# Mixer projections with high and low rows side by side, and GpSimd scaling the gates

## The reference, cut to what matters

```python
def hybrid_mixer(h, w_in, b_forget, g_kv, w_kv_up, g_idx_k, w_up_fox, w_up_sb, w_up_dsa, w_out, cos, sin):
    (q_a, k_a, v_a, f_a, q_b, k_b, v_b, q_c, c_kv, q_i, k_i, w_i, gates) = split(h @ w_in)
    y_a = forgetting_attention(heads(q_a), heads(k_a), heads(v_a), f_a + b_forget)
    y_b = stick_breaking_attention(heads(q_b), heads(k_b), heads(v_b))
    k_c, v_c = split(rmsnorm(c_kv, g_kv) @ w_kv_up, 2)
    ...                                   # rotations, index scores, top-k selection
    y_c = dsa_attention(q_c, k_c, v_c, q_i, k_i, w_i)
    g_a, g_b, g_c = split(sigmoid(gates), 3)
    merged = g_a * (y_a @ w_up_fox) + g_b * (y_b @ w_up_sb) + g_c * (y_c @ w_up_dsa)
    return merged @ w_out

for l in range(2):
    x = x + 0.5 * swiglu(rmsnorm(x, g_ffn1[l]), ...)
    x = x + hybrid_mixer(rmsnorm(x, g_mix[l]), w_in[l], ...)
    x = x + 0.5 * swiglu(rmsnorm(x, g_ffn2[l]), ...)
```

## Time and profile before

| | |
|---|---|
| time, median of 3 runs | 2421.66 us (2421.42 to 2421.71) |
| span of the profiled execution | 2420.2 us, 1.4 us under the median |
| PE busy | 2401.0 us, 99% |
| DVE busy | 1556.3 us, 64% |
| ACT busy | 1216.8 us, 50% |
| POOL busy | 359.8 us, 15% |
| chain that ended last | PE 96%, DVE 2%, ACT 1% |
| PE's granted clock | 0.9 or more of full speed in each of 40 slices |

### The profile page before, as it was taken

One profiled execution on the slowest core, in us unless ns is written; L12 is line 12 of the kernel. 1 busy time (PEld: TensorE's weight loads), 2 busy tenths in 40 slices (PEclk: granted clock), 3 DMA queues, 4 the chain that ended last, 5 costly groups with the idle time before them and its releaser, 6 DMA issues.

```text
span 2420.2 us, 37041 instructions
## 1 busy us (share of the span) xinstructions
PE 2401.0 (99%) x14600; PEld 2057.4 (85%) x14600; DVE 1556.3 (64%) x2659; ACT 1216.8 (50%) x2220; POOL 359.8 (15%) x340
## 2 busy tenths in 40 slices
PE   8999999999999999999999999999999999999998
PEld 6766689888888877988888899998888889999887
DVE  5335455663455556677688677578767767757875
ACT  4344444322222546565566545566656554556654
POOL 0343322000001235200100000240010010024000
PEclk9999999999999999999999999999999999999999
DMA  6334423443454422455655554355565564435554
GB/s 279 132 113 157 157 87 122 160 168 134 157 169 140 152 94 98 149 185 173 203 202 181 180 177 136 117 191 190 171 212 175 175 200 150 148 110 199 190 175 137
DMA packets 88605, 389.96 MB, mean 161 GB/s; under 512 B 15025, under 2 KB 27601, under 8 KB 58353
## 3 DMA queue, kind: packets, MB, share of 16 engines
q1 hardware_dynamic: 81232, 356.07, 43.3%
q0 software_dynamic: 7200, 31.52, 3.7%
HBM read 386.52 MB, written 1.05 MB: 160 GB/s over the span
## 4 chain that ended last, share of the span: by engine, by line
PE 96%; DVE 2%; ACT 1%; issue 0%; DMA 0%; POOL 0%; SPq 0%; DVEq 0%; POOLq 0%; ACTq 0%
PE ps L1243 43%; PE ps L1283 38%; PE ps L1479 3%; PE ps L1542 2%; PE ps L1553 2%; PE ps L1568 2%; PE ps L1377 1%; PE ps L1392 1%; DVE ring_lo L2217 1%; PE ps L1523 0%; ACT logits L1951 0%; DMA arena<-w_mod 0%; PE ps L1346 0%; PE ps L1411 0%; ACT w_hi L1718 0%
## 5 line engine op out<-in xcount | busy, mean ns | idle before, releaser
L2217 DVE TENSOR_TENSOR ring_lo<-ring,w_hi 128x1024 fp32r<-128x1024 f32 (+4 forms) x708 | 777.4, 1124 | 202.8 <-ACT w_hi L1718 200.1
L1718 ACT ACTIVATE w_hi<-ring 128x1024 fp32r<-128x1024 f32 (+4 forms) x708 | 634.3, 944 | 290.0 <-PE ps L1243 199.1
L1243 PE MATMUL ps<-h_hi,w_hi 128*128 128x256 f32 (+1 forms) x1632 | 500.1, 332 | 1.9 <-ACT arena L1841 1.2
L1243 PE MATMUL ps<-h_lo,w_hi 128*128 128x256 f32 (+1 forms) x1632 | 487.9, 324 | 0.1
L1283 PE MATMUL ps<-h_hi,w_hi 128*128 128x512 f32 x1760 | 446.3, 393 | 0.6 <-DVE h_hi L2390 0.3
L1283 PEld LDWEIGHTS ps<-h_hi,w_hi 128*128 128x128 f32 x1760 | 316.2, 189 | 57.6 <-issue 1.5
L1243 PEld LDWEIGHTS ps<-h_hi,w_hi 128*128 128x128 f32 x1632 | 307.1, 190 | 38.3 <-issue 12.2
L1243 PEld LDWEIGHTS ps<-h_lo,w_hi 128*128 128x128 f32 x1632 | 307.5, 190 | 24.2 <-DVE h_lo L2518 0.4
L1243 PE MATMUL ps<-h_hi,ring_lo 128*128 128x256 f32 (+1 forms) x1632 | 307.1, 325 | 0.3 <-DVE ring_lo L2217 0.3
L1243 PEld LDWEIGHTS ps<-h_hi,ring_lo 128*128 128x128 f32 x1632 | 250.3, 190 | 28.5 <-issue 2.2
L1283 PEld LDWEIGHTS ps<-h_hi,ring_lo 128*128 128x128 f32 x1760 | 242.4, 190 | 18.3 <-DVE ring_lo L2217 0.6
(11 more groups left out here) (298 smaller groups left out, 2900.3 us busy)
## 6 DMA issues: line engine op xcount, KB each, us to landing
ring<-w_ffn_in SPq DMA_DIRECT2D x132, 1024.0 KB, 4.8
ring<-w_ffn_out SPq DMA_DIRECT2D x96, 704.0 KB, 4.1
ring<-w_in SPq DMA_DIRECT2D x36, 1024.0 KB, 4.8
ring<-w_w_in SPq DMA_DIRECT2D x26, 1024.0 KB, 4.9
bias_t<-w_mod POOLq DMA_DIRECT2D x24, 1024.0 KB, 5.3
ring<-w_mod SPq DMA_DIRECT2D x16, 1024.0 KB, 6.2
ring<-w_up SPq DMA_DIRECT2D x16, 576.0 KB, 3.7
ring<-w_pab SPq DMA_DIRECT2D x8, 1024.0 KB, 4.9
```

The source lines that it names most:

```text
L1243: mm = pe.matmul(ps[fs[k].bank][:, at_col:at_col + n], (hi_w if wpart == "hi" else lo_w)[0:rows, at[k]:at[k] + P], hi if part == "hi" else ...
L1718: act.activation(w_hi[q.s % 2][:, h * n:(h + 1) * n], ring[q.slot][:, h * n:(h + 1) * n], ACT.Copy)\
L2217: dve.tensor_tensor(ring_lo[q.slot][:, c], ring[q.slot][:, c], plain(w_hi[q.s % 2][:, c]), ALU.subtract)\
```

## The change

In the mixers of the second block the feature and gate tiles now use `product_wide`. So that it finds its rows, the layer ahead writes the mixer's rows side by side ("wide" in place of "defer"), and the token-wise projections read them from there. Per tile there are 8 matmuls of 512 columns and 8 of 256 in place of 24 of 256. The insertions keep about their place in time: the numbers in the tables are changed to count the longer matmuls.

Taking a tile out has new steps. ACT copies columns 256 to 511 of the bank into `spare` (two buffers; it also waits until DVE has taken the tile two before). DVE waits for that copy and adds the halves. For a feature tile DVE then multiplies by `row` in a second instruction that waits for the first. For a gate tile POOL multiplies by `row`, one tile later in its stream, and the Sigmoid waits for it. The gates of branch 1 move from `h_hi` to `h_lo`, since `h_hi` is now full.

```diff
@@ hybrid_kernel
-        gate_lo = over("gates_b", KC * S, h_at + 4 * KC * S, F32)
+        gate_lo = over("gates_b", KC * S, l_at, F32)
@@ feat
+                mix = {}
+                if name[0] == "2":
+                    mix = dict(mix=count("mix"), free=mixed[-2] if len(mixed) > 1 else None, gate=last_gate[0] if name[1] == "g" else None)
+                    mixed.append(f)
+                    if name[1] == "g":
+                        last_gate[0] = (c, f, count("gate_row"))
@@ second_block
-            ffn(w["ffn1_in"][l], w["ffn1_out"][l], "half", None, ("defer", v("g_mix", 8 * l, 8)), fresh=plan.counts["h"],
+            ffn(w["ffn1_in"][l], w["ffn1_out"][l], "half", None, ("wide", v("g_mix", 8 * l, 8)), fresh=plan.counts["h"],
...
-            among(t, lambda: {13: [turned((feat2, 12 * S, 0), 1, fc(12))], 20: [turned((feat2, 13 * S, 0), 0, fc(13))]})
+            among(t, lambda: {7: [turned((feat2, 12 * S, 0), 1, fc(12))], 13: [turned((feat2, 13 * S, 0), 0, fc(13))]})
...
-            among(t, lambda: {12: stick_z(0, 1)})
+            among(t, lambda: {6: stick_z(0, 1)})
...
-            among(t, lambda: {20: stick_z(4)})
+            among(t, lambda: {13: stick_z(4)})
@@ pe_feat
-                if st["tiles"]:
+                if st["tiles"] and st["name"][0] == "2":
+                    product_wide(st["tiles"], [(st["p"], [(c * P * st["n"] + st["i"] * P, h_hi[:, c * SQ:(c + 1) * SQ], c) for c in range(KC)])],
+                                 st["fresh"], mids=st.get("mids", {}))
+                elif st["tiles"]:
@@ act_feat
                 if st["name"][0] == "2":
+                    full(f)
+                    if st["free"]:
+                        taken(st["free"])
+                    act.activation(spare[:, st["mix"] % 2 * S:(st["mix"] % 2 + 1) * S], ps[f.bank][:, S:SQ], ACT.Copy).then_inc(mix_half, 1)
                     return
@@ act_merge2, open_gates
+                    act.wait_ge(gate_row, st["gate_row"] + 16 + m + 1)
@@ gpsimd
+            def gate_by_row(gate):
+                if gate:
+                    c, f, _ = gate
+                    taken(f)
+                    pool.tensor_tensor(gates2(c), gates2(c), row[:, 0:S], ALU.mult).then_inc(gate_row, 1)
@@ dve_feat
-                if not gate and (c < 3 or 6 <= c < 9 or 12 <= c < 15):
-                    ins = dve.scalar_tensor_tensor(dst, ps[f.bank][:, 0:S], SCALE, row[:, 0:S], ALU.mult, ALU.mult)
-                else:
-                    ins = dve.tensor_tensor(dst, ps[f.bank][:, 0:S], row[:, 0:S], ALU.mult)
+                dve.wait_ge(mix_half, st["mix"])
+                ins = dve.tensor_tensor(dst, ps[f.bank][:, 0:S], spare[:, st["mix"] % 2 * S:(st["mix"] % 2 + 1) * S], ALU.add)
+                if not gate:
+                    link(ins)
+                    if c < 3 or 6 <= c < 9 or 12 <= c < 15:
+                        ins = dve.scalar_tensor_tensor(dst, dst, SCALE, row[:, 0:S], ALU.mult, ALU.mult)
+                    else:
+                        ins = dve.tensor_tensor(dst, dst, row[:, 0:S], ALU.mult)
```

More of the change, by code:

```diff
@@ L1209, in run, with within @@
                     mm.then_inc(piece_begun, 1)
+            def within(its):
+                for what, it in its if isinstance(its, list) else [its]:
+                    dict(sums=pe_sums, spread=pe_spread, att=pe_att, head_spread=pe_head_spread, rope=pe_rope, kvup=pe_kvup,
+                         index=pe_index, stick_z=pe_stick_z, unread=lambda u: between(dict(unread=u), 0))[what](it)
             def product(fs, n, groups, fresh=None, need=None, at_col=0, mids={}, more=False, hold=False, odd=None):
@@ L1238, in product @@
                         if at_mm in mids:
[L1239 to L1241 removed]
+                            within(mids[at_mm])
                         at_mm += 1
@@ L1474, in pe_tok @@
                                 c, at = j * per + i, i * cols
-                                for part in parts:
+                                for part in range(1 if low else 2):
                                     if at_mm in mids:
@@ L1478, in pe_tok @@
                                     at_mm += 1
-                                    mm = pe.matmul(ps[f.bank][:, 0:st["n"]], at_T(part, c, T, t * P, P), wt[:, at:at + st["n"]],
-                                                   start=c == 0 and part is h_hi and not low, stop=c == KC - 1 and low)
+                                    rows = at_T(h_hi, c, SQ, part * S + t * P, P) if T == S else at_T(h_lo if part else h_hi, c, T, t * P, P)
+                                    mm = pe.matmul(ps[f.bank][:, 0:st["n"]], rows, wt[:, at:at + st["n"]],
+                                                   start=c == 0 and part == 0 and not low, stop=c == KC - 1 and low)
                                     run(p, mm)
```

40 lines of the change are left out of this document (22 added, 18 removed).

## The result

The changed kernel takes 2436.57 us (median of 5 runs, 2436.32 to 2437.0), the one before 2421.57 us (5 runs beside them, 2421.0 to 2421.71). The ratio is 1.0062, with a 95% interval of 1.0051 to 1.0073: 0.6% slower, 3.2 us above the forecast of 2433.4 and within its range. The profiled execution spans 2434.5 us, 14.3 more than before.

A forecast was written before the change was run, and what follows sets the result against it. PE was taken to set the time nearly everywhere. Waits of 1.35 + 5.95 + 0.4 = 7.7 us a layer, less 1.8 kept in gate tiles, leave 5.9, 11.8 in both: span 2432.0, median 2433.4 us, range 2423 to 2443.

The forecast's parts named there:

- PE's gain: Feature and gate tiles: a row chunk costs 348.4 ns, before 357.9; 9.5 ns less, 6.2 us in all.
- The turn: Turn of chunk 12: three feature tiles' second DVE instructions end L2571 later; PE's rotation waits the whole 1.35 us.
- The stick-breaking chain: Index scores through `va`: copies behind Abs and Exp make masks and splits late; PE waits 5.95 us a layer.
- term 2.1: PE 2.1 us behind at the mask of head 2, the index scores' 0.4 us included.
- term 3.85: Through `va`: PE waits 3.05 us for ACT's split of the second piece, then 0.8 us for DVE's.
- The start of the attention: Among the gate tiles: DVE now waits for the copy as well; 0.4 us a layer (0 to 0.45).
- POOL: Gate tiles: 48 products of about 0.92 us, 22 us a layer, fit; cost put at nothing.
- The contention rival: DVE's splits and POOL's products: ten meet on the critical path at 0.92 us, adding 9 us: 2442.6; chance 0.07.
- The sign that the prediction names: The forecast is wrong if, among other signs, DVE's splits grow longer beside POOL's products.
- What ACT gets: Mixer: 82 copies of 383 ns, 31.4 us; the work fits, but a copy waits for its tile and behind insertions.
- All hidden: Rival: every new step fits into idle time and PE keeps its 6.2 us: 2415.5 us; chance 0.12.
- Only DVE's second instruction: Rival: copies cost nothing further down; PE waits 2.7 us a layer at chunk 12, head 2 and `va`: 2423.5; chance 0.15.

The follow-up runs named there:

- the experiment: Changed kernel with early Sigmoids, tenth gate tile in the old way, only feature tiles 15, 11, 16, 17 in the new: 2419.74 us, ratio 0.9992 to the kernel before.
- the kernel with neither step: Changed kernel without ACT's copies and without DVE's second instruction in the feature tiles: 2417.40 us, ratio 0.9982 to the kernel before.

## Why the forecast held, and which terms were off

- **What bounds the kernel.** Right: PE's stream sets the time, and the loss is idle time that others give it.
- **PE's gain.** The 9.5 ns a row chunk came out somewhat lower: 9.2 between neighbouring gate tiles, 8.5 over all 24 (1.62 us a layer against 1.8). "The feature tiles' own gain is lost in those waits": right. At the turn a part is even seen as such (0.24 us).
- **The turn.** Right in place and cause. The term was 1.35 us and measured 1.39 for the three instructions. PE's lost gain of 0.24 stands on top, as the forecast had counted the gain as lost.
- **The stick-breaking chain.** Right in mechanism: the copy behind Abs and Exp, DVE idle for it, the masks and then both halves of the split late. Undoing only that order brought 8.9 us back. The stretch up to the scores of head 4 cost 2.5 us with the index scores (term 2.1), and that through `va` 3.9 (term 3.85). That the latter comes so close is partly luck. The clock had not been thought of, and did no harm only because PE's slower matmuls were spent in a wait. The forecast also had PE wait 3.05 us at the second piece alone; in layer 1, where the clock stayed up, it waited 1.07 us at the first and 1.64 at the second.
- **The start of the attention.** 0.48 us, against 0.4 with a bound of 0.45. The forecast named no tile; when I named one for the experiment, it was the wrong one.
- **POOL.** Right at nothing, but the reading of the earlier trace rows beside it was wrong. The 950 ns there are a mean of splits of 0.75 us and of splits of up to 1.3 us behind a POOL instruction, so contention is 0.5 us where it strikes, and not 0.2. The contention rival failed on its count: it had ten products meet a split on the critical path, and two meet one, off that path. The sign that the prediction names (splits that grow longer beside POOL's products) did appear in those two, and cost nothing. The products took 0.74 to 0.78 us on average, not the 0.92 of the row I had taken.
- **What ACT gets.** This is the step that failed, though the time stayed within the range. "In the steady part that follows the copies fall into ACT's idle time" holds until the last gate tile. There the copy turns a queue that ran ahead of PE into one that waits for it, with the table load and the Sigmoids behind. I had looked for what stands ahead of the copies, and not for what stands behind the last one. It cost 1.16 us a layer, 2.3 of the 3.3 us that the two layers' sum of 11.8 fell short of the measured 15.1.
- **The layer's first tile.** The wait for the low rows, 0.2 us a layer, has no term in the prediction.
- **The rivals.** "All hidden" (2415.5) is refuted by the time; the kernel with neither step, which has nothing to hide, takes 2417.4. "Only DVE's second instruction" was worked out as 2423.5, and the kernel without copies gives 2423.2. So its price was right, but it is not the whole: the copies by themselves cost 12.0 us.

## What to carry to other kernels

An instruction that takes a result out of an accumulator on another engine has two prices: its duration, and its place in that engine's queue. Here 383 ns of work fitted easily, but in three feature tiles of a layer the copy stood behind two or four activations, and that place alone cost 4.4 us a layer, over ten times one copy's duration. Before such a copy is added, look at what stands ahead of it (who waits for it meanwhile) and at what stands behind it (what had been done early and now waits for PE), first of all a table load. When an engine gets faster by tenths of a microsecond, its suppliers were often only just in time: count the gain only over stretches without a supplier's wait.

## What the runs showed of the hardware

- The same gap of 2.12 to 2.14 us on PE stands in both layers of four kernels here: the changed one, the one with narrow gate tiles, the one without POOL's products and the one with the early Sigmoids alone. In each the granted clock fell behind one of the two gaps (to 0.5 to 0.58 in stretches of 2 us, the 1.2 GHz level) and stayed at 1.00 behind the other: in the first and the third the low clock came in layer 0, in the other two in layer 1. In the changed kernel both layers took the same time, since PE would have waited behind it.
- A DVE split with two operands in SBUF (576 columns) took 0.75 us by itself and 1.29 to 1.30 us when POOL's add of 256 columns was under way as it started. That add took 0.74 us by itself and 1.07 to 1.24 us when such a split was under way as it started. The mean of the group, 982 ns, hides both.
- The same `ACTIVATE` copy of 256 columns took 375 ns on average, near the 383 of the row it was priced from.
